# A decoder layer on one core: two value blocks moved behind projection units, two into the attention, and GpSimd's quarter passes begun later

## The reference

```python
x = layer_norm(x, emb_ln_g, emb_ln_b)
u_pool, q, c, iq, ik, iw = split(x @ w_in)          # 512, 8x64, 128, 8x64, 64, 8 columns
pool_out = per_group_map(trailing_mean(u_pool, windows 2, 4, 8, 16) - u_pool) * pool_scale
q_lat = einsum(q, w_uk)                             # 8 heads, 128 latent columns
c = rms_norm(c, kv_norm_g)                          # one latent of 128 for keys and values
score[t, s] = sum_h iw[t, h] * relu(iq[t, h] . ik[s]); keep the 256 largest causal ones
p = softmax(q_lat . c / 8 + rel_bias[bucket(t - s)]) over the kept ones
attn = (p @ c) @ w_uv                               # per head
x = layer_norm(ALPHA * x + concat(pool_out, attn) @ w_o, ln1_g, ln1_b)
x = layer_norm(ALPHA * x + relu(x @ w_up) ** 2 @ w_down, ln2_g, ln2_b)
```

## Time and profile before

| | us |
|---|---|
| median of 3 runs | 1254.53 |
| lowest, highest | 1252.13, 1254.89 |
| the profiled execution, its own time | 1251.68 |
| its span, first to last instruction | 1249.9 |
| mean granted TensorE clock | 0.992 of full speed |
| TensorE busy | 1192.2 |
| VectorE busy | 852.5 |
| ScalarE busy | 540.0 |
| GpSimd busy | 518.3 |

### The profile page before, as it was taken

The page is one execution under the profiler, slowest core; times in us unless marked ns, Lnnn a source line. Parts: engine busy times, 40 slices in busy tenths (PEclk is TensorE's granted clock), DMA queues, the critical chain, the costliest instruction groups (busy, mean ns, idle before and its releaser), DMA issues.

```text
span 1249.9 us, 16263 instructions
## 1 busy us (share of the span) xinstructions
PE 1192.2 (95%) x5551; PEld 959.6 (77%) x5551; DVE 852.5 (68%) x1291; ACT 540.0 (43%) x875; POOL 518.3 (41%) x420
## 2 busy tenths in 40 slices
PE   5999999789999999999999989979899999999997
PEld 4776686568788778778788778968788888888886
DVE  6388986887857888888988878857533333333357
ACT  4545633665165244244244266642342442433440
POOL 2235764945335676776775653222002102103002
PEclk9999999999999999999999999999999999999999
DMA  7723431021314333242243300044233332323331
GB/s 224 251 77 100 154 89 64 1 68 34 102 35 135 96 107 118 84 127 92 86 132 100 97 5 1 2 146 123 77 92 100 103 101 88 115 97 88 118 101 68
DMA packets 126852, 118.63 MB, mean 95 GB/s; under 512 B 5773, under 2 KB 99530, under 8 KB 126794
## 3 DMA queue, kind: packets, MB, share of 16 engines
q1 hardware_dynamic: 126794, 117.86, 30.4%
HBM read 107.34 MB, written 10.50 MB: 94 GB/s over the span
## 4 chain that ended last, share of the span: by engine, by line
PE 79%; POOL 9%; DVE 6%; issue 3%; ACT 2%; DMA 1%; POOLq 0%; DVEq 0%; SPq 0%; ACTq 0%
PE g_bank L1644 15%; PE g_bank L1646 15%; PE g_bank L1645 15%; PE wide L1644 8%; PE wide L1646 8%; PE wide L1645 8%; POOL wlo L454 3%; PE g_bank L1802 3%; PE g_bank L1604 2%; POOL rows L864 1%; PE wide L1708 1%; PE wide L1709 1%; POOL mask L829 1%; DVE logit L1063 1%; POOL emb_stage L856 1%
## 5 line engine op out<-in xcount | busy, mean ns | idle before, releaser
L454 POOL TENSOR_TENSOR wlo<-wring,whi 128x1024 fp32r<-128x1024 f32 (+1 forms) x94 | 229.5, 2442 | 221.4 <-ACT whi L1508 123.4
L1644 PE MATMUL g_bank<-xhi,whi 128*128 128x512 f32 (+2 forms) x768 | 301.5, 393 | 4.8 <-DVE xlo L695 3.8
L1646 PE MATMUL g_bank<-xhi,wlo 128*128 128x512 f32 (+2 forms) x768 | 297.6, 387 | 0.0
L1645 PE MATMUL g_bank<-xlo,whi 128*128 128x512 f32 (+2 forms) x768 | 297.5, 387 | 0.0
L1508 ACT ACTIVATE whi<-wring 128x1024 fp32r<-128x1024 f32 x120 | 127.1, 1059 | 355.9 <-PE wide L1646 179.8
L454 DVE TENSOR_TENSOR wlo<-wring,whi 128x1024 fp32r<-128x1024 f32 (+1 forms) x66 | 84.4, 1278 | 197.8 <-ACT whi L1508 192.7
L1644 PE MATMUL wide<-whi,hhi 128*128 128x512 f32 x480 | 190.2, 396 | 0.8 <-POOL wlo L454 0.8
L1646 PE MATMUL wide<-whi,hlo 128*128 128x512 f32 x480 | 189.6, 395 | 0.0
L1645 PE MATMUL wide<-wlo,hhi 128*128 128x512 f32 x480 | 189.6, 395 | 0.0
L1644 PEld LDWEIGHTS g_bank<-xhi,whi 128*128 128x128 f32 (+1 forms) x768 | 144.6, 188 | 39.9 <-DVE xlo L695 4.3
L1645 PEld LDWEIGHTS g_bank<-xlo,whi 128*128 128x128 f32 (+1 forms) x768 | 144.7, 188 | 32.9 <-issue 1.8
(11 more groups left out here) (238 smaller groups left out, 1931.7 us busy)
## 6 DMA issues: line engine op xcount, KB each, us to landing
wring<-in_w_up SPq DMA_DIRECT2D x64, 512.0 KB, 4.1
wring<-in_w_down SPq DMA_DIRECT2D x64, 512.0 KB, 3.7
wring<-in_w_in SPq DMA_DIRECT2D x26, 512.0 KB, 3.7
wring<-in_w_o SPq DMA_DIRECT2D x16, 512.0 KB, 4.0
rows<-in_x SPq DMA_DIRECT2D x8, 512.0 KB, 5.0
normalized_rows<-rows SPq DMA_DIRECT2D x8, 512.0 KB, 6.7
rows<-normalized_rows SPq DMA_DIRECT2D x4, 512.0 KB, 5.0
emb_stage<-normalized_rows SPq DMA_DIRECT2D x4, 512.0 KB, 4.9
```

The costliest lines, as they stand in the source:

```text
L454: eng.tensor_tensor(parts_of(name, lo_tile(name)), parts_of(name, wring[n % 4]), parts_of(name, hi_tile(name)).bitcast(F32), ALU.subtract) ...
L1644: nc.tensor.matmul(out_ap, w_hi, m_hi, start=first, stop=False)
L1645: nc.tensor.matmul(out_ap, w_hi, m_lo, start=False, stop=False)
L1646: return nc.tensor.matmul(out_ap, w_lo, m_hi, start=False, stop=last)
```

## The change

1. In chunk 0 the blocks `vv0` and `vv1` are formed behind the projection units u1 and u2. For that the first 256 columns of the latents get split parts of their own, `latT0_hi` and `latT0_lo`, made behind the latents' transposes. They lie in the place of `work`, so VectorE waits for the product of `vv1` ahead of `select_pair`.
2. The blocks `vv2` and `vv3` are formed inside the first attention: at the steps 4 and 8 on TensorE and ScalarE (`MID_VALUES`), and on VectorE one step later, behind `mask_logits(5)` and `mask_logits(9)`.
3. At the beginning of the attention only the other 256 columns are split: by ScalarE where the 512 were, by VectorE behind `mask_logits(1)`.
4. GpSimd's quarter passes begin behind mask 6 (the seventh) in place of mask 0. The last six come behind the last spread of reciprocals.

```diff
-    order = ("u0 u1 u2 po0 u3 po1 q0 po2 q1 po3 q2 q3", "q0 q1 q2 u0 u1 u2 po0 u3 po1 q3 po2 po3")[c]
+    order = ("u0 u1 vv0 u2 vv1 po0 u3 po1 q0 po2 q1 po3 q2 q3", "q0 q1 q2 u0 u1 u2 po0 u3 po1 q3 po2 po3")[c]
...
+    if not c and step in MID_VALUES:
+        out += [("vv", 0, MID_VALUES[step])]
...
+MID_VALUES = {4: 2, 8: 3}
...
+        latT0_hi = part("latT0_hi", 84.25, [P, 2 * P], F32R)
+        latT0_lo = part("latT0_lo", 85.25, [P, 2 * P], F32R)
...
-                    if c == 0:
-                        emb_gains(m)
+                    if c == 0 and m >= 6:
+                        emb_gains(m - 6)
                 spread_reciprocals(8 * c + 7)
+                for m in range(26, 32) if c == 0 else ():
+                    emb_gains(m)
...
-                    if step == 32 * c:
-                        for k in ((0, 1, 2, 3), (2, 3, 4, 5, 6, 7))[c]:
-                            values_lo(c, k)
+                    if step == 1:
+                        latents_lo(1)
+                    if step - 1 in MID_VALUES:
+                        values_lo(0, MID_VALUES[step - 1])
+                    if c and step == 32:
+                        for k in range(2, NB):
+                            values_lo(1, k)
...
+            latents_lo(0)
             pooled = pooling(dve, 0, chain)
             normalized = normalize(EMB1, 1)
             for n in range(8):
...
                 add_score(2 * n)
                 add_score(2 * n + 1)
+                if 1 <= n <= 2:
+                    values_lo(0, n - 1)
...
+            dve.wait_ge(g_full, EV[("vv", 0, 1)])
             select_pair()
...
+                if c == 0:
+                    act.wait_ge(g_evac, EV[("cT", 0)])
+                    nc.scalar.activation(latT0_hi[:, :], latT[:, 0:2 * P], ACT.Copy).then_inc(latT_hi_ready, 1)
...
                 exps(lo)
-                for k in ((0, 1, 2, 3), (2, 3, 4, 5, 6, 7))[c]:
-                    values_hi(c, k)
+                for k in range(2, NB) if c else ():
+                    values_hi(1, k)
                 for step in range(lo, lo + LAST_STEP):
                     if step + 1 < hi:
                         exps(step + 1)
                     for name in attention_step(c, step):
                         ps = bank(name)
-                        if name[0] == "tr":
+                        if name[0] == "vv":
+                            values_hi(0, name[2])
+                        elif name[0] == "tr":
...
-            nc.scalar.activation(latT_hi[:, 0:CHUNK], latT[:, 0:CHUNK], ACT.Copy).then_inc(latT_hi_ready, 1)
+            nc.scalar.activation(latT_hi[:, 2 * P:4 * P], latT[:, 2 * P:4 * P], ACT.Copy).then_inc(latT_hi_ready, 1)
...
-                            pe.wait_ge(v_lo_ready, VALUES[("vv", c, (3, 5)[c] if i < 6 else 7)])
+                            pe.wait_ge(v_lo_ready, VALUES[("vv", c, (i, 5 if i < 6 else 7)[c])])
```

More of the change, by code:

```diff
@@ L107, in psum_uses @@
         names += [("ql", 1, h) for h in range(HEADS)] if c else []
-        names += [("vv", c, k) for k in ((0, 1, 2, 3), (2, 3, 4, 5, 6, 7))[c]]
+        names += [("vv", 1, k) for k in range(2, NB)] if c else []
         names += attention(c) + [("proj", c, nh, b) for nh in range(2) for b in range(CB)]
@@ L389, in layer @@
             units += [("ik", c), ("c", c)] + [("iq", c, p) for p in range(4)]
-            units += [name for name in tokens_queries(c) if name[0] != "po"]
+            units += [name for name in tokens_queries(c) if name[0] in ("u", "q")]
         for c in range(2):
@@ L1081, in latents_lo @@
             def latents_lo(c):
-                at = slice(0, CHUNK * (c + 1))
+                at = (slice(0, 2 * P), slice(2 * P, 4 * P), slice(0, S))[c]
+                hi_part, lo_part = (latT_hi[:, at], latT_lo[:, at]) if c else (latT0_hi[:, :], latT0_lo[:, :])
                 dve.wait_ge(latT_hi_ready, c + 1)
-                nc.vector.tensor_tensor(latT_lo[:, at], latT[:, at], latT_hi[:, at].bitcast(F32), ALU.subtract)\
-                    .then_inc(latT_lo_ready, 1)
+                nc.vector.tensor_tensor(lo_part, latT[:, at], hi_part.bitcast(F32), ALU.subtract).then_inc(latT_lo_ready, 1)
             def latent_query_lo(h):
@@ L1247, in _ @@
             dve.wait_ge(masks01_ready, 2)
-            latents_lo(0)
             attention(0)
@@ L1255, in _ @@
                 select(i)
-            latents_lo(1)
+            latents_lo(2)
             for h in range(HEADS):
@@ L1392, in products @@
                     n = name[2]
+                    if name[0] == "vv":
+                        values_hi(0, n)
+                        continue
                     if name[0] == "po":
@@ L1725, in products @@
                 for name in tokens_queries(c):
+                    if name[0] == "vv":
+                        values(0, name[2])
+                        continue
                     if name[0] == "po":
@@ L1742, in values @@
                 at = slice(k * P, k * P + P)
+                early = c == 0 and k < 2
+                hi_part, lo_part = (latT0_hi, latT0_lo) if early else (latT_hi, latT_lo)
                 pe.wait_ge(wuv_lo_ready, 1)
-                pe.wait_ge(latT_lo_ready, c + 1)
+                pe.wait_ge(latT_lo_ready, 3 if c else 1 if early else 2)
                 free(name)
-                three_passes(bank(name)[:, :], latT_hi[:, at], latT_lo[:, at], wuv_hi[:, :], wuv_lo[:, :], True, True)\
+                three_passes(bank(name)[:, :], hi_part[:, at], lo_part[:, at], wuv_hi[:, :], wuv_lo[:, :], True, True)\
                     .then_inc(g_full, 1)
@@ L1776, in attention @@
                     pe.wait_ge(relu_ready, 48)
-                    pe.wait_ge(latT_lo_ready, 2)
+                    pe.wait_ge(latT_lo_ready, 3)
                 logits(lo)
                 logits(lo + 1)
-                for k in ((0, 1, 2, 3), (2, 3, 4, 5, 6, 7))[c]:
-                    values(c, k)
+                for k in range(2, NB) if c else ():
+                    values(1, k)
                 pe.wait_ge(cells_zero, 8 * c + 8)
@@ L1806, in attention @@
                             last.then_inc(pv_full, 1)
+                        elif name[0] == "vv":
+                            values(0, name[2])
                         elif name[0] == "rT":
```

## The result

The changed kernel takes 1255.43 us (median of 17 runs, 1253.52 to 1257.29), the kernel before in the same series 1252.53 (17 runs, 1248.89 to 1254.89). The ratio is 1.0020, with a 95% interval from 1.0012 to 1.0028: 1.5 to 3.5 us slower, with 2.5 in the middle. The forecast was +1.80, and 1256.3 between 1252.2 and 1259.3. The profiled execution of the changed kernel has a span of 1253.9 in a time of 1255.96, so this one is 4.0 above the profiled execution of before.

The account below looks back on a forecast made before the run. TensorE was taken as the bound, full in chunk 0's projections but with holes in the attention. The terms 1.40 + 0.50 - 3.20 + 3.40 - 1.00 + 0.50 + 0.20 gave +1.80: 1256.3 us, range 1252.2 to 1259.3.

Parts of the forecast that it names:

- Two early blocks: Chunk 0's projections: two blocks behind u1 and u2, 0.70 of TensorE matmuls each, all on the path, +1.40.
- Stall of q0: Chunk 0: q0 waits for its bank until VectorE's value split of vv1 ends, +0.50, from 0 to 0.9.
- late `add_score`: Rival, chunk 0: GpSimd's weight split holds the second add_score for 2.40 and q0 with it; +4.2, 1258.7, chance 0.11.
- The opening: Start of the first attention: without four value splits, mask_logits(1) waits only for GpSimd's second mask; -3.20 at step 5.
- Middle blocks: Attention steps 4 and 8: VectorE's split waits for both ScalarE copies, delaying probs_lo; 1.70 a block, +3.40 for two.
- The passes: Attention behind step 7: GpSimd, its passes moved, gets ahead and no longer delays masks; -1.00, between 0.4 and 1.5.
- First pool_lo split: Start of the projection behind attention: VectorE's first split waits for part of a GpSimd pass; +0.50, from 0 to 1.3.
- The clock: Opening: TensorE, nearly without work from 215 to 219, might fall to 1.2 GHz, costing about 1.2; +0.20 put in.
- A granted clock under 1.00 between 213 and 240: Sign, in the opening and first attention steps, that would show the forecast wrong; no size given.
- the middle blocks hide: Rival, steps 5 and 9: VectorE's waits fall into lost time, 3.4 becomes 1.3, sum -0.3; chance 0.14 for faster.
- The moved passes do nothing: Rival, attention: GpSimd wasn't the limit, so the 1.00 is missing; +2.8, 1257.3, chance 0.09.
- The clock falls: Rival, opening or the holes in steps 5 and 9: +1.2 each, sum +3.0 to +4.2, 1257.5 to 1258.7; chance 0.12.

Follow-up runs that it names:

- vv1_later: The changed kernel with the second early block behind po0 instead of ahead of it; from the last iq copy to the qT copy 55.01 us, 1.42 above before.
- passes_alone: The kernel before with only GpSimd's quarter passes moved, from the seventh mask on and six behind the last spread of reciprocals; 0.9987 of before.
- late_split: The changed kernel with VectorE's split of the two middle blocks behind probs_lo, not in front of it; 1.1 us below the changed kernel at equal clock.
- two_opening: The changed kernel with the blocks of steps 4 and 8 formed in the opening, behind logits(1); 1.8 us below the changed kernel at equal clock.
- warm_opening: The changed kernel with 18 transposes of the identity on TensorE behind logits(1), their result overwritten; ratio 1.0012 to the kernel before.
- passes_ahead_alone: The kernel before with GpSimd's passes from the seventh mask on and the last six ahead of the last spread of reciprocals; ratio 0.9974.

## Why the prediction came out right, point by point

The forecast was +1.80 and the ratio says +2.5; the 1255.43 lies within both stated ranges (1254.5 to 1258.0 and 1252.2 to 1259.3). It was to be within 0.2% with a chance of 0.54, and it is at the edge of that: 0.20%. The terms, each with what it measured:

- *Two early blocks, +1.40*: 1.42. *Stall of q0, +0.50*: 0.43, and shown by `vv1_later`. The late `add_score` (0.11) didn't come: the pair started at 84.91 and GpSimd's split at 86.48.
- *The opening, -3.20*: -3.09 at full clock (8.08 to 4.99).
- *Middle blocks, +3.40*: 2.81. The first cost 1.75, as sized (1.70). The second cost only 1.06 net: its own cycle is as long (4.34), but the two waits let GpSimd get ahead, and it comes back in the cycle from step 15 to 17: 3.19 in place of the 3.87 of `passes_alone`, where VectorE waits for the masks of the steps 16 and 17. The mechanism, both copies of ScalarE in front of VectorE's split, is shown by the two later splits.
- *The passes, -1.00*: -0.75. VectorE waits for no mask from step 9 to 17 in the changed kernel, as I said. What I had written into this term, that the slow cycles let GpSimd get ahead, is in the 0.6 by which the second block is cheaper. The two terms together were +2.40 and are +2.06.
- *First pool_lo split, +0.50*: +0.57 in one execution, +0.27 in the other.
- *The clock, +0.20*: +0.97 in the opening. **This is the mis-sized term.** I had given the fall a chance of 0.12 and put 0.2 into the sum. Eight profiles have TensorE's hole of 2.57 to 2.60 there (two of the changed kernel, six of others), and seven of them show the fall; only `late_split` has none. `two_opening`, with six of the twelve matmuls left, fell behind a hole of 1.57, and `warm_opening` behind the first middle block. The four profiles with all twelve matmuls show no fall there. The size I gave, some 1.2, was near; the odds were wrong. I had argued that a hole of 1.48 stood there without a fall; the new hole is 2.59. A granted clock under 1.00 between 213 and 240 was on my own list of what would show the forecast wrong, and it came: in this point the forecast failed, and the range held because one fall costs only 0.97.
- Steps 17 to 31: I had nothing there, and it is +0.15 to 0.2 in the kernels with two middle blocks and two early ones. All of it lies in the cycle from step 19 to 21 (3.85 in place of 3.66). Its cause is open.

The sum of the measured terms is 1.42 + 0.43 - 3.09 + 2.81 - 0.75 + 0.57 + 0.97 + 0.15 = +2.51. Without the clock's 0.97 it is +1.54, against +1.60 forecast without the 0.20: that agreement owes something to errors that cancel, 0.59 on the middle blocks against 0.25 on the passes, 0.11 on the opening and 0.15 that I didn't have.

Of the 4.0 between the first two profiles, 0.42 was there before that stretch of chunk 0 began (59.72 against 59.30; the changed kernel's second profile has 59.30), and some 0.8 comes from the start of chunk 1, where the clock stayed low for longer:

```profile
126.00:132.00 6.00, 3.59 (x15) 2.34 (x16) 6.00 (x18) 5.79 (x9) 5.31 (x5) 0.73 0.56 214
132.00:138.00 6.00, 6.00 (x20) 3.42 (x19) 6.00 (x18) 2.86 (x5) 3.96 (x4) 0.70 1.00 369
```

The second profile of before has 1.00 in 132 to 138. But `passes_alone` and `passes_ahead_alone`, whose code is that of before up to there, have 0.82 and 0.76. From the last `qT` copy to the first mask step the five profiles without early blocks take 104.20 to 105.60, the nine with them 103.86 to 105.31. These lie over each other, so I don't count this to the change, though both profiles of the changed kernel (105.17, 105.31) are above both of before (104.36, 104.20).

The rivals: "the middle blocks hide" is wrong, their cost per block is far from 0.1. "The moved passes do nothing" is wrong. "The clock falls" is what happened, once and not twice: no fall stood at steps 5 and 9 of the changed kernel, whose holes are 1.5 long.

## What to carry to other kernels

An engine's copy or split that is inserted into a pipeline costs little by its length and much by its place: put it where its input is already there. Here the same split cost 1.4 us a block right behind the step that feeds it, and 0.5 two steps later. Work that a waiting engine does in its own queue in front of a spread or a reciprocal is free if it ends in time; the same six passes behind that wait met a VectorE step that needs the same SBUF access. And matmuls taken out of a wait may be what keeps TensorE's clock up: count a fall of the clock as a term of its own when a hole grows. To find out what the rest of a change costs, compare kernels at the same mean granted clock; to find out what the change costs in all, don't, since a fall that it brings is then taken out too.

## What the runs showed of the hardware

The scatter of this kernel's times goes mostly with TensorE's clock. Executions had mean granted clocks from 0.986 to 0.998, within one kernel up to 0.010 apart, and 0.79 us of time went with each 0.001. In the attention and at the start of the projection, falls of the clock stood behind or in holes of TensorE of 1.5 to 2.6 us, but not always (at the start of chunk 1 every profile has one, among holes of 0.7 to 0.9): with an idle time of 2.59 before 219.02 `late_split` had none, and the changed kernel fell at the start of the projection in one execution and not in the next. Filling one hole with 18 transposes (2.13 us) kept the clock up there in the one profile that was taken, and it fell at the next hole, 1.5 us long, behind which it stayed at 1.00 in the changed kernel.
